# Low-rank time-mix products on scaled weights, a one-engine evacuation of the normed rows, and a wait moved behind filler transposes

## The reference, cut to what matters

```python
xf = xn.astype(F32)                     # normed rows, 256 x 1024
x_prev = jnp.pad(xf[:, :-1], ((0, 0), (1, 0), (0, 0)))
xx = x_prev - xf                        # the shifted difference
xr, xw, xk, xv, xa, xg = [xf + xx * mu[i] for i in range(6)]
r, k, v = xr @ wr, xk @ wk, xv @ wv
w_log = -jax.nn.softplus(-(w0 + jnp.tanh(xw @ w1) @ w2)) - 0.5    # w1: 1024 x 64
a = jax.nn.sigmoid(a0 + (xa @ a1) @ a2)                           # a1: 1024 x 64
g = jax.nn.sigmoid(xg @ g1) @ g2                                  # g1: 1024 x 160
```

## Time and profile before

| what | value |
|---|---|
| median of 3 runs | 1568.73 us |
| lowest, highest | 1564.68, 1569.08 us |
| profiled execution, its own time | 1557.25 us |
| its span, first to last instruction | 1555.2 us |
| mean granted TensorE clock | 0.996 of full speed |
| PE busy / DVE / ACT | 98% / 81% / 64% |

### The profile page before, as it was taken

One profiled execution on the slowest core, in us unless ns is written; L12 is line 12 of the kernel. 1 busy time (PEld: TensorE's weight loads), 2 busy tenths in 40 slices (PEclk: granted clock), 3 DMA queues, 4 the chain that ended last, 5 costly groups with the idle time before them and its releaser, 6 DMA issues.

```text
span 1555.2 us, 21510 instructions
## 1 busy us (share of the span) xinstructions
PE 1521.9 (98%) x7832; PEld 1257.1 (81%) x7832; DVE 1264.2 (81%) x1449; ACT 997.4 (64%) x1139; POOL 9.3 (1%) x10
## 2 busy tenths in 40 slices
PE   8999999899999999999999999999999999999997
PEld 5678888589889767888888888888888888888885
DVE  3456666866866259999999999999999999999997
ACT  2244444553422138887887887878888888887886
POOL 0000000000000010000000000000000000000000
PEclk9999999999999999999999999999999999999999
DMA  9779443024003649999999999999999999999970
GB/s 362 286 277 300 163 162 109 0 82 140 22 1 110 227 176 400 397 377 363 387 366 358 387 361 359 385 381 343 383 381 344 381 379 349 376 379 357 370 292 27
DMA packets 203269, 439.36 MB, mean 283 GB/s; under 512 B 7217, under 2 KB 44337, under 8 KB 203090
## 3 DMA queue, kind: packets, MB, share of 16 engines
q1 hardware_dynamic: 200434, 434.05, 76.4%
q10 hardware_dynamic: 2208, 2.50, 0.5%
q0 software_dynamic: 576, 2.10, 0.3%
HBM read 427.09 MB, written 11.53 MB: 282 GB/s over the span
## 4 chain that ended last, share of the span: by engine, by line
PE 94%; DVE 3%; ACT 1%; issue 1%; DMA 0%; DVEq 0%; ACTq 0%
PE psum L1494 19%; PE psum L1496 19%; PE psum L1495 19%; PE psum L567 6%; PE psum L2227 5%; PE psum L2229 3%; PE psum L2155 2%; PE psum L842 2%; PE psum L2200 2%; PE psum L1512 2%; PE psum L2211 1%; PE psum L2213 1%; PE psum L2212 1%; PE psum L738 1%; PE psum L728 1%; PE psum L643 1%
## 5 line engine op out<-in xcount | busy, mean ns | idle before, releaser
L1694 DVE TENSOR_TENSOR w_lo<-ring,w_hi 128x1024 fp32r<-128x1024 f32 x672 | 805.0, 1221 | 51.5 <-ACT w_hi L1598 11.4
L1598 ACT ACTIVATE w_hi<-ring 128x1024 fp32r<-128x1024 f32 x672 | 711.4, 1062 | 186.6 <-PE psum L1496 186.4
L1494 PE MATMUL psum<-w_hi,xg_split 128*128 128x512 f32 x896 | 353.5, 395 | 0.4 <-DVE xg_split L1788 0.4
L1496 PE MATMUL psum<-w_lo,xg_split 128*128 128x512 f32 x896 | 349.4, 390 | 0.0
L1495 PE MATMUL psum<-w_hi,xg_split 128*128 128x512 f32 x896 | 348.8, 389 | 0.0
L1496 PEld LDWEIGHTS psum<-w_lo,xg_split 128*128 128x128 f32 x896 | 168.2, 188 | 35.7
L1494 PEld LDWEIGHTS psum<-w_hi,xg_split 128*128 128x128 f32 x896 | 168.2, 188 | 34.1 <-DVE xg_split L1788 0.6
L1495 PEld LDWEIGHTS psum<-w_hi,xg_split 128*128 128x128 f32 x896 | 168.4, 188 | 33.6
L1494 PE MATMUL psum<-w_hi,ht_split 128*128 128x512 f32 x448 | 176.0, 393 | 1.7 <-DVE w_lo L1694 1.7
L1496 PE MATMUL psum<-w_lo,ht_split 128*128 128x512 f32 x448 | 174.5, 390 | 0.0
L1495 PE MATMUL psum<-w_hi,ht_split 128*128 128x512 f32 x448 | 174.3, 389 | 0.0
(11 more groups left out here) (332 smaller groups left out, 1558.4 us busy)
## 6 DMA issues: line engine op xcount, KB each, us to landing
ring<-o_moe_wg_dram SPq DMA_DIRECT2D x56, 2048.0 KB, 9.1
ring<-o_moe_wu_dram SPq DMA_DIRECT2D x56, 2048.0 KB, 9.2
ring<-o_moe_wd_dram SPq DMA_DIRECT2D x56, 2048.0 KB, 9.1
ring<-e_ffn_wg_dram SPq DMA_DIRECT2D x11, 1024.0 KB, 5.5
ring<-e_ffn_wu_dram SPq DMA_DIRECT2D x11, 1024.0 KB, 8.7
ring<-e_ffn_wd_dram SPq DMA_DIRECT2D x11, 1024.0 KB, 10.6
expert_rows<-work SPq DMA_DIRECT2D x1, 8192.0 KB, 29.4
ring<-e_w_in_dram SPq DMA_DIRECT2D x2, 2048.0 KB, 18.1
```

Source lines behind the costliest of these rows:

```text
L1494: nc.tensor.matmul(dst, x_hi, hi, start=first, stop=False)
L1496: return nc.tensor.matmul(dst, x_hi, lo, start=False, stop=last_)
L1598: nc.scalar.activation(w_hi[:, (4 * i + n) % 4, :], piece(i, n), ACT.Copy).then_inc(m_hi, 1)
L1694: V.tensor_tensor(w_lo[:, r, :], piece(i, n), w_hi[:, r, :].bitcast(F32), ALU.subtract).then_inc(m_lo, 1)
```

## The change

The low-rank products of w and a are no longer taken of mixed inputs. Since (xf + xx * mu) @ w1 = xf @ w1 + xx @ (mu * w1), VectorE scales the rows of w1 and a1 by their mu (two instructions, 128 x 8 x 64, ahead of `add_to_h`), and TensorE accumulates xnT on the plain weights and then xx on the scaled ones. w1 and a1 lie side by side as one 128-column weight `wa1`, so one bank holds both results: w in partitions 0 to 63, a in 64 to 127. The a2 product therefore reads partitions 64 to 127. Two of VectorE's six mixed inputs fall away. ScalarE alone takes all eight slices of `xnT` out; VectorE computes the four pairs of `xx` at once. The two products of g1 alternate slice by slice. The 16 filler transposes become 6. ScalarE's `hi_x(0)` and `hi_w(2)` move behind its eight sigmoids of a. In the scan, TensorE's wait for the zeroings goes behind the 22 filler transposes.

```diff
@@ -397,13 +397,13 @@
-        w1s = wu(2, 512).rearrange("p (k n) -> p k n", k=KT)
-        a1s = wu(2, 512, 512).rearrange("p (k n) -> p k n", k=KT)
+        wa1, wa1_mu = r3(wu(2, 1024), KT), r3(wu(2, 1024, 1024), KT)
+        w1s, a1s = wa1[:, :, 0:64], wa1[:, :, 64:P]
...
-        mix = [r3(wu(u), KT) for u in (0, 1, 0, 1, 0, 4)]
+        mix = [r3(wu(u), KT) for u in (0, 1, 0, 4)]
-        MIX = (1, 4, 5, 0, 2, 3)
+        MIX = (5, 0, 2, 3)
...
-                             (w2s[64:65, :], I["o_w0"]), (a2s[0:64, :], two("o_a2")), (g2a, g2[0:P, :]),
+                             (w2s[64:65, :], I["o_w0"]), (a2s[64:P, :], two("o_a2")), (g2a, g2[0:P, :]),
-            for _ in range(16):
+            for _ in range(6):
                 nc.tensor.transpose(psum[:, 3, 0:P], ident, ident)
 
-            norm_ready(pe, 2)
...
-            product(0, [(w1s[:, k, :], mix[0][:, k, :]) for k in range(KT)], 64, mixed=0)
-            product(1, [(a1s[:, k, :], mix[1][:, k, :]) for k in range(KT)], 64, mixed=1)
-            product(2, [(g1s[:, k, 0:P], mix[2][:, k, :]) for k in range(KT)], mixed=2)
-            product(3, [(g1s[:, k, P:160], mix[2][:, k, :]) for k in range(KT)], 32)
+            for k in range(KT):
+                pe.wait_ge(n_eva, 8 + k + 1)
+                nc.tensor.matmul(psum[:, 0, 0:T], wa1[:, k, :], xnT[:, k, :], start=(k == 0), stop=False)
+            pe.wait_ge(lora_rhs, 2)
+            for k in range(KT):
+                pe.wait_ge(lora_rhs, 2 + k // 2 + 1)
+                last = nc.tensor.matmul(psum[:, 0, 0:T], wa1_mu[:, k, :], xx[:, k, :], start=False, stop=(k == KT - 1))
+            last.then_inc(o_mm, 2)
+            for k in range(KT):
+                pe.wait_ge(mix_ready, k + 1)
+                for n, (cols_, rows) in enumerate(((slice(0, P), P), (slice(P, 160), 32))):
+                    last = nc.tensor.matmul(psum[0:rows, 2 + n, 0:T], g1s[:, k, cols_], mix[0][:, k, :], start=(k == 0),
+                                            stop=(k == KT - 1))
+                    if k == KT - 1:
+                        last.then_inc(o_mm, 1)
...
-                product(8 + k, [(a2s[0:64, k * P:(k + 1) * P], ta[0:64, :])])
+                product(8 + k, [(a2s[64:P, k * P:(k + 1) * P], ta[64:P, :])])
-            pe.wait_ge(y_zero, 3)
             pe.wait_ge(a_ma, 16)
             for _ in range(22):
                 nc.tensor.transpose(psum[:, 2, 0:P], ident, ident)
+            pe.wait_ge(y_zero, 3)
         def rwkv_act(act):
             root_table()
             norm_act(act, 2)
-            norm_cols(2, "o_norm_mix")[0](act)
+            for k in range(KT):
+                act.wait_ge(n_tr, 8 + k // 2 + 1)
+                nc.scalar.activation(xnT[:, k, :], psum[:, 4 + k // 2, (k % 2) * T:(k % 2 + 1) * T], ACT.Copy,
+                                     scale=col("o_norm_mix", k)).then_inc(n_eva, 1)
...
-                act.wait_ge(mix_ready, KT * (4 + i))
-                nc.scalar.activation(q_x(i, 1), mix[3 + i].rearrange("p k t -> p (k t)"), ACT.Copy).then_inc(q_hi, 1)
+                act.wait_ge(mix_ready, KT * (2 + i))
+                nc.scalar.activation(q_x(i, 1), mix[1 + i].rearrange("p k t -> p (k t)"), ACT.Copy).then_inc(q_hi, 1)
...
-                    i_ = nc.scalar.activation(ta[0:64, :], ps[0:64, 0:T], ACT.Copy)
+                    i_ = nc.scalar.activation(ta[64:P, :], psum[64:P, 0, 0:T], ACT.Copy)
                 i_.then_inc(o_act, 1)
-                if n == 7:
-                    hi_x(0)
-                    hi_w(2)
+            hi_x(0)
+            hi_w(2)
             hi_x(1)
             hi_w(3)
-            norm_cols(2, "o_norm_mix")[1](dve)
+            dve.wait_ge(f_last, 4)
             nc.vector.tensor_scalar(omk, col("o_k_a", 0, 8), -1.0, 1.0, ALU.mult, ALU.add)
             nc.vector.memset(tw[64:65, :], 1.0).then_inc(ones_row, 1)
-            dve.wait_ge(f_last, 4)
...
             def stepped(q):
-                if q % 2 == 0:
-                    dve.wait_ge(n_eva, 8 + q + 2)
-                else:
-                    dve.wait_ge(n_evd, 8 + q + 1)
+                dve.wait_ge(n_eva, 8 + 2 * q + 2)
                 ks = slice(2 * q, 2 * q + 2)
                 nc.vector.tensor_tensor(xx[:, ks, 1:], xnT[:, ks, 0:T - 1], xnT[:, ks, 1:], ALU.subtract)
-                link(dve, "dve", nc.vector.tensor_scalar(xx[:, ks, 0:1], xnT[:, ks, 0:1], -1.0, None, ALU.mult))
+                nc.vector.tensor_scalar(xx[:, ks, 0:1], xnT[:, ks, 0:1], -1.0, None, ALU.mult).then_inc(lora_rhs, 1)
 
             def mixed(j):
                 if j >= 2:
-                    dve.wait_ge(o_mm, (1, 2, 4, 24)[j - 2])
+                    dve.wait_ge(o_mm, (4, 24)[j - 2])
                 for k in range(KT):
                     if j == 0 and k % 2 == 0:
-                        stepped(k // 2)
+                        dve.wait_ge(lora_rhs, 2 + k // 2 + 1)
                     nc.vector.scalar_tensor_tensor(out=mix[j][:, k, :], in0=xx[:, k, :],
                                                    scalar=col("o_mu", 8 * MIX[j] + k), in1=xnT[:, k, :],
...
-            for j in range(5):
+            for q in range(4):
+                stepped(q)
+            for j in range(3):
                 mixed(j)
...
-            mixed(5)
+            mixed(3)
                     hidden(NFC - 1)
                     hidden_lo(NFC - 1)
+            dve.wait_ge(lora_in, 16 * 9)
+            dve.wait_ge(f_hT, NFC)
+            for w, at, m in ((w1s, 0, 1), (a1s, 64, 4)):
+                mu = col("o_mu", 8 * m, KT).unsqueeze(2).to_broadcast([P, KT, 64])
+                nc.vector.tensor_tensor(wa1_mu[:, :, at:at + 64], w, mu, ALU.mult).then_inc(lora_rhs, 1)
             add_to_h(dve, f_last, (1, 2, 3, 4), 2)
```

More of the change, by code:

```diff
@@ L201, in trunk @@
         s_wo, s_h = sem("out_proj"), sem("h_added")
-        f_gate, f_last = sem("ffn_gate_sum"), sem("ffn_down_bank")
+        f_gate, f_last, lora_rhs = sem("ffn_gate_sum"), sem("ffn_down_bank"), sem("lora_scaled_and_steps")
         f_sil, f_h = sem("ffn_silu"), sem("ffn_hidden")
@@ L553, in rwkv_pe, with product @@
             norm_pe(pe, 2, 8)
-            for _ in range(16):
+            for _ in range(6):
                 nc.tensor.transpose(psum[:, 3, 0:P], ident, ident)
-            norm_ready(pe, 2)
             pe.wait_ge(lora_in, 16 * 9)
             pe.wait_ge(f_h, NFC)
-            def product(n, lhs_rhs, rows=P, width=T, mixed=None):
+            def product(n, lhs_rhs, rows=P, width=T):
                 if n >= 8:
@@ L564, in product @@
                 for i, (l, r) in enumerate(lhs_rhs):
-                    if mixed is not None:
-                        pe.wait_ge(mix_ready, KT * mixed + i + 1)
                     last = nc.tensor.matmul(psum[0:rows, n % 8, 0:width], l, r, start=(i == 0), stop=(i == len(lhs_rhs) - 1))
@@ L1089, in lo_x @@
                 dve.wait_ge(q_hi, QAT["x", i])
-                nc.vector.tensor_tensor(q_x(i, 0), mix[3 + i].rearrange("p k t -> p (k t)"), q_x(i, 1).bitcast(F32),
+                nc.vector.tensor_tensor(q_x(i, 0), mix[1 + i].rearrange("p k t -> p (k t)"), q_x(i, 1).bitcast(F32),
                                         ALU.subtract).then_inc(q_lo, 1)
             V = nc.vector
-            for j in range(5):
+            for q in range(4):
+                stepped(q)
+            for j in range(3):
                 mixed(j)
@@ L1120, in rwkv_dve @@
             link(dve, "dve", last)
-            dve.wait_ge(mix_ready, 6 * KT)
+            dve.wait_ge(mix_ready, 4 * KT)
             V.tensor_tensor(sqT, kk, kk, ALU.mult).then_inc(k_sq, 1)
```

## The result

| | before | after |
|---|---|---|
| median | 1566.7 us (4 executions, 1564.31 to 1569.08) | 1550.22 us (4, 1549.36 to 1551.5) |
| ratio | | 0.9896, 95% interval 0.9879 to 0.9914 |
| profiled execution, its own time | 1557.25 us | 1550.25 us |
| its span | 1555.2 us | 1548.3 us |
| mean clock in the profiled execution | 0.996 | 0.998 |

The forecast was 1560.5 us, 1556.0 to 1565.2. (A fourth execution of before, 1564.31 us, brings its median from 1568.73 to 1566.7.) Between the two profiled executions, though, the difference is 7.0 us. So the first question is not where the change saves time but why most executions of the kernel before take 7 to 12 us longer than the one that was profiled.

A forecast was written before the change was run, and what follows sets the result against it. TensorE, carrying 94% of the chain, was taken to bound the kernel; low-rank stage 3.6 us (2.6 + 1.0) plus first solve 4.65 us gave 8.25 us off the median 1568.73, so 1560.5 us, range 1556.0 to 1565.2.

The forecast's parts named there:

- Start of the low-rank stage, 2.7 us: Low-rank stage: with six fillers and only slice 0 needed, the first product starts at 281.4 for 284.08, 2.7 us earlier.
- the scaling: Low-rank stage: two VectorE weight scalings, 1.4 us, fit its 1.79 us wait for TensorE and cost nothing; uncovered, 1.4 us.
- the difference hidden: Low-rank stage: VectorE's xx pairs and g's mixed input are ready before TensorE asks, first pair wanted at 284.9; no cost.
- g1 in turns, 9.4 us, the two together 2.6: Low-rank stage: alternating g1 takes 9.4 us instead of 7.0; with the earlier start, w2 starts at 297.8, gaining 2.6 us.
- The first solve, 4.65 us: Scan's first solve: fillers run before the zeroing ends, so L719 starts at 433.05 instead of 437.75; 4.65 us gained.
- The rival of a clock that falls there: First solve: the clock falls all the same, losing 2.5 of the 4.65 us; 1563.0 us, chance 0.10.
- ScalarE's two conversions moved, 1.0 us: Low-rank stage: sigmoids of a keep pace, so TensorE's 1.00 us wait before g2 goes; 1.0 us gained.
- the 8.25: Whole kernel: 3.6 us from the low-rank stage plus 4.65 from the first solve, taken off the median 1568.73 us.
- the rival for *slower: Low-rank stage: with ten fillers missing the clock falls and stays at 1.2 GHz through the first products; 1576.9 us, chance 0.03.
- The rival of a gain taken back at the expert stage's head: Only one place pays, an unseen wait, likely the experts' weight stream, taking gain back; 1565.1 or 1564.1 us, chance 0.07.
- an end of the scan less than 7 us earlier: Scan: a sign that the forecast is wrong, its end coming forward by less than 7 us.

The follow-up runs named there:

- g1_block: The change with g1's two products in two blocks instead of taking turns; 1550.28 us, ratio to before 0.9902.
- lora_only: The change without its last hunk, so TensorE's wait for the zeroings stands ahead of the 22 filler transposes again; 1554.3 us, ratio to before 0.9942.
- after_again: The change itself measured once more, in another group; 1549.53 us, ratio to before 0.9893.
- solve_only: The kernel before with only TensorE's wait for the zeroings moved behind the 22 filler transposes; 1561.56 us, ratio to before 0.9982.
- after_conversions_back: The change with ScalarE's two conversions put back behind result 7 of its sigmoids of a; 1557.91 us, ratio to before 0.9956.
- before_g2_block: The kernel before with g2's products in two blocks, eight of 128 rows, then eight of 32; 1556.93 us, ratio to before 0.9953.
- after_g2_block: The change with only g2's products in two blocks, g1's still in turns; 1548.42 us, ratio to before 0.9905.
- before_sigmoids_first: The kernel before with only ScalarE's two conversions moved behind the eight sigmoids of a; 1556.68 us, ratio to before 0.9952.
- g12_block: The change with both g1's and g2's products in two blocks; 1544.81 us, ratio to before 0.9875.

## Why the prediction was wrong

- **Start of the low-rank stage, 2.7 us**: right (281.51 for 281.4), with ScalarE ahead all the way, the scaling and the difference hidden.
- **g1 in turns, 9.4 us, the two together 2.6**: right (9.39; w2 at 297.74). g1_block measures the turns' price by themselves: 9.39 - 7.19 = 2.2 us.
- **The first solve, 4.65 us**: right. 4.74 in the profile; by medians 1554.3 (lora_only) less 1549.5 (after_again) is 4.8. The rival of a clock that falls there is out (1.00 in 425 to 441). The rule of the Trainium skill ("TensorE: Matmul & The Clock Gate", Part 4) that the full clock does not engage for transposes, by which that rival would have been the forecast, is not borne out: the clock stayed at 1.00 through the 22 filler transposes (2.62 us, L713).
- **ScalarE's two conversions moved, 1.0 us**: this is the term that failed. The wait ahead of g2 was found, but it was priced at its length. What it brings with it, a clock that usually falls within g2, was put at nothing. The term measured 7.7 us on the kernel before and 7.7 to 8.4 on the change, of which 1.0 is the wait and 6.7 or more the clock.
- With it the sum reads 2.6 + 7.7 + 4.7 = 15.0 us, and after_again stands 14.9 us below the 1564.44 beside it. The low-rank part of it, 2.6 + 7.7 = 10.3, is lora_only's 10.35. What the first comparison's 16.5 has beyond that is mostly the luck of the few executions of before in it: their median, 1566.7, and the 1568.73 from which I took the 8.25, lie 2.3 and 4.3 us above the medians of 11 to 27 executions.
- **What let it pass** was a sentence further on: "That execution stands 0.7% under the median 1568.73, to which I apply the same 8.25". 0.7% is 11.5 us, more than the whole forecast, and I did not ask where they were. The three runs shown (1564.68 to 1569.08) all lay above the profiled 1557.25: the profile was of an execution that the kernel seldom has. A price taken from it holds only for an execution like it.
- I had argued a low clock in the low-rank stage as the rival for *slower*, as something that the change might bring. By the mean clocks it was there already, in most executions, a little further on (g2 and the cumulative products), and the change took it away.
- The rival of a gain taken back at the expert stage's head did not come about in the change (the first expert product comes 6.9 us earlier, the span is 6.9 us shorter); in g1_block it did, by the clock, with TensorE busy 10.00 of 10.00 us in 556 to 566.
- Among the signs of being wrong was an end of the scan less than 7 us earlier. The 6.9 us in after just meets it, but it is the dip at 315 and not a fault in the solve: without the dip, in after_again, it is 8.6.

## What to carry to other kernels

When the profiled execution lies well off the timed ones, the difference has a place in the program, and an edit may be worth that difference rather than the wait that the profile shows; look for it in the mean clock of each execution before pricing anything. A TensorE wait of a microsecond is not always worth a microsecond: here the clock usually fell behind one of 1.0 us between products of 64 rows and g2's turns, and it cost 7.7 us, so that even filling it with useless work paid 6.0. Others of about that length, 1.34 us idle in 282 to 284 and 0.98 us at the first solve of the change, left the clock full; what sets them apart is not shown. Products that alternate between two shapes took 2.2 and 2.6 us more than the same products as two blocks, so blocks are worth trying; whether the whole kernel gains has to be measured (g1_block did not).

## What the runs showed of the hardware

- An idle time of 1.0 us ahead of g2 was followed 2.3 to 2.6 us after its end by a clock at 1.2 GHz for 17 us, with TensorE busy throughout (profiles of solve_only and after_conversions_back); the mean clocks of most executions of before fit it. The profiled execution of before had the wait and no fall. In the idle time of 3.78 us at the first solve the clock fell at 431.2 and stayed low for 6.8 us. How long a fall lasts went with what was run behind it: 17 us with g2 in turns, 7 with g2 in blocks (before_g2_block, one profile).
- The clock also fell with no idle time near: for 3.4 us in the change (315 to 319) and in after_g2_block (313 to 316), and for 17 us in one execution of before_sigmoids_first. What starts those is open; other kernels have slower executions at a lower mean clock now and then (lora_only three of ten at 1561.7 to 1562.1 with 0.991, g12_block one of six at 1551.5 with 0.993), whose place no profile shows.
- A change of shape between float32 products cost nearly the same whether the contraction or the columns changed: 2.2 us for the fifteen changes within g1 (128 and 32 columns) against one, 10.0 - 7.4 = 2.6 us for those within g2 (128 and 32 rows).
